# Gate weights and gate inputs of the first recurrence in two parts: three products of 256 columns for each float32 product

## What is computed

```python
def rg_lru(x, w_a, b_a, w_x, b_x, lam):
    xb = x.reshape(B, S, RG_BLOCKS, RG_BLOCK_DIM)
    r = jax.nn.sigmoid(jnp.einsum('bsnc,ncd->bsnd', xb, w_a).reshape(B, S, C) + b_a)
    i = jax.nn.sigmoid(jnp.einsum('bsnc,ncd->bsnd', xb, w_x).reshape(B, S, C) + b_x)
    log_a = -RG_C * r.astype(jnp.float32) * jax.nn.softplus(-lam.astype(jnp.float32))
    a = jnp.exp(log_a)
    mult = jnp.sqrt(-jnp.expm1(2.0 * log_a))
    b = mult * (i * x).astype(jnp.float32)
    _, h = lax.associative_scan(combine, (a, b), axis=1)   # h = a * h_before + b
```

## Time and profile before

| what | value |
|---|---|
| median of 3 runs | 1200.94 us (1200.78 to 1202.69) |
| profiled execution | 1200.8 us |
| its span, first to last instruction | 1199.0 us |
| its mean granted TensorE clock | 0.998 |
| PE, PEld busy | 1181.3 us (99%), 1160.6 us (97%) |
| DVE, ACT, POOL busy | 849.5 us (71%), 713.8 us (60%), 441.5 us (37%) |
| recorded PE products | 10128 |

### The profile page before, as it was taken

How to read it: one execution, slowest core, us unless ns; L and a number is a source line. 1 busy time by engine, 2 the same in 40 slices (tenths; PEclk the granted TensorE clock), 3 DMA queues, 4 the chain that set the end, 5 groups by cost and what they waited for, 6 DMA issues and landing times.

```text
span 1199.0 us, 27004 instructions
## 1 busy us (share of the span) xinstructions
PE 1181.3 (99%) x10128; PEld 1160.6 (97%) x10128; DVE 849.5 (71%) x1399; ACT 713.8 (60%) x1242; POOL 441.5 (37%) x415
## 2 busy tenths in 40 slices
PE   8999999999999999999999999999999999999997
PEld 7999999999999999999999999999999999999996
DVE  5868665676877764878667877755877677877754
ACT  5767667545766654566456666645566456666643
POOL 3007315123344402232338534423622349444422
PEclk9999999999999999999999999999999999999999
DMA  7554445654655666454554655566544554665563
GB/s 260 184 165 159 132 157 164 192 192 159 194 192 192 188 189 197 158 161 147 181 189 140 203 189 193 179 196 182 160 162 155 188 173 151 201 197 191 180 201 100
DMA packets 60286, 212.61 MB, mean 177 GB/s; under 512 B 6688, under 2 KB 7968, under 8 KB 60064
## 3 DMA queue, kind: packets, MB, share of 16 engines
q1 hardware_dynamic: 60192, 211.32, 55.9%
HBM read 210.24 MB, written 1.05 MB: 176 GB/s over the span
## 4 chain that ended last, share of the span: by engine, by line
PE 89%; DVE 5%; issue 2%; ACT 2%; POOL 1%; POOLq 0%; DVEq 0%; ACTq 0%
PE bank L1101 28%; PE bank L1103 28%; PE bank L1102 28%; DVE wlo L1400 2%; PE bank L1117 1%; PE bank L1249 1%; PE bank L1218 1%; ACT whi L766 1%; PE bank L1229 1%; PE bank L1273 1%; DVE prob L1565 1%; DVE prob L1540 0%; POOL u L683 0%; DVE u L1632 0%; PE bank L1158 0%
## 5 line engine op out<-in xcount | busy, mean ns | idle before, releaser
L1400 DVE TENSOR_TENSOR wlo<-raw,whi 128x1024 fp32r<-128x1024 f32 (+1 forms) x400 | 499.9, 1250 | 204.2 <-ACT whi L766 202.5
L1101 PE MATMUL bank<-shifted,whi 128*128 128x256 f32 x2296 | 639.0, 278 | 1.5 <-POOL shifted L702 1.1
L1102 PE MATMUL bank<-shifted,whi 128*128 128x256 f32 x2296 | 636.2, 277 | 0.0
L1103 PE MATMUL bank<-shifted,wlo 128*128 128x256 f32 x2296 | 635.8, 277 | 0.0
L766 ACT ACTIVATE whi<-raw 128x1024 fp32r<-128x1024 f32 (+1 forms) x400 | 416.5, 1042 | 149.4 <-PE bank L1103 137.9
L1101 PEld LDWEIGHTS bank<-shifted,whi 128*128 128x128 f32 x2296 | 431.6, 188 | 3.4 <-POOL shifted L702 1.3
L1103 PEld LDWEIGHTS bank<-shifted,wlo 128*128 128x128 f32 x2296 | 431.7, 188 | 0.0
L1102 PEld LDWEIGHTS bank<-shifted,whi 128*128 128x128 f32 x2296 | 431.1, 188 | 0.0
L662 POOL TENSOR_TENSOR fprod<-ugate,uval 128x256 f32<-128x256 f32 x66 | 95.5, 1447 | 197.5 <-DVE uval L1715 188.2
L1101 PE MATMUL bank<-fhi,whi 128*128 128x256 f32 x528 | 145.8, 276 | 0.0
L1102 PE MATMUL bank<-flo,whi 128*128 128x256 f32 x528 | 145.7, 276 | 0.0
(11 more groups left out here) (218 smaller groups left out, 1258.7 us busy)
## 6 DMA issues: line engine op xcount, KB each, us to landing
raw<-in_w_win SPq DMA_DIRECT2D x140, 512.0 KB, 3.5
raw<-in_w_up SPq DMA_DIRECT2D x132, 512.0 KB, 3.5
raw<-in_w_down SPq DMA_DIRECT2D x48, 448.0 KB, 3.5
raw<-in_w_merge SPq DMA_DIRECT2D x32, 512.0 KB, 3.6
raw<-in_w_out SPq DMA_DIRECT2D x24, 512.0 KB, 4.3
raw<-in_w_down SPq DMA_DIRECT2D x24, 512.0 KB, 3.5
x<-in_x SPq DMA_DIRECT2D x4, 256.0 KB, 4.5
rgw<-in_rg_w SPq DMA_DIRECT2D x1, 1024.0 KB, 10.1
```

The lines of the kernel that those rows point to most:

```text
L1101: pe.matmul(ps, whi[:, slot, w], hi, start=first, stop=False)
L1102: pe.matmul(ps, whi[:, slot, w], lo, start=False, stop=False)
L1103: return pe.matmul(ps, wlo[:, slot, w], hi, start=False, stop=last)
L1400: dve.tensor_tensor(wlo[:, n % RING, w], raw[:, n % RING, w], whi[:, n % RING, w].bitcast(f32), ALU.subtract) \
```

## The change

The gate weights and the eight input tiles are split as all other operands are. `gate_weights(part)` lays the parts over tiles of `yhi` and `ylo` that are not in use until later (eight tiles of each, seen as 16 blocks of 128x128); the parts of the input tiles take turns in `yhi[13]`, `yhi[14]` and `ylo[13]`, `ylo[14]`. ACT copies the weights in two halves of 128x1024 in slots 3 and 4 and tile t in slot 3 + 2t; DVE subtracts the weights' halves in slots 3 and 4 and tile t in slot 4 + 2t. PE's wait of a gate step is now for these parts, and it makes six products in place of two float32 ones. `load_rg` is waited for by ACT, and by PE only at the later `pool_mix`.

```diff
+    for i in range(2):
+        at(3 + i, "rg_weights", i)
     for t in range(KT):
+        at(3 + 2 * t, "rg_x_high", t)
+        at(4 + 2 * t, "rg_x_low", t)
         at(6 + 2 * t, "rg_gates", t)
...
+        def gate_weights(part):
+            at = 17 + 14 * part
+            return shifted[:, at:at + KT, :].rearrange("p t s -> p (t s)").rearrange("p (b n) -> p b n", n=P)
...
# ACT
+            def step_rg_weights(i):
+                if i == 0:
+                    act.wait_ge(load_rg, 32)
+                w = slice(KT * i, KT * (i + 1))
+                act.activation(gate_weights(0)[:, w, :], rgw[:, w, :], ACT.Copy).then_inc(rgw_hi, 1)
+
+            def step_rg_x_high(t):
+                act.wait_ge(conv_done, t + 1)
+                if t >= 2:
+                    act.wait_ge(misc_done, MISC[("rg_gates", t - 2)] + 1)
+                act.activation(yhi[13 + t % 2], u1[:, XR + t, :], ACT.Copy).then_inc(rg_x_hi, 1)
...
# PE
             def step_rg_gates(t):
                 u = MISC[("rg_gates", t)]
                 if t == 0:
-                    pe.wait_ge(load_rg, 32)
-                pe.wait_ge(conv_done, t + 1)
+                    pe.wait_ge(rgw_lo, 2)
+                pe.wait_ge(rg_x_lo, t + 1)
                 wait(pe, misc_read, u)
+                hi, lo = yhi[13 + t % 2], ylo[13 + t % 2]
                 for g in range(2):
-                    mm = pe.matmul(ps_misc[:, g * S:(g + 1) * S], rgw[:, g * KT + t, :], u1[:, XR + t, :], start=True, stop=True,
-                                   skip_group_check=True)
+                    ps, b = ps_misc[:, g * S:(g + 1) * S], g * KT + t
+                    pe.matmul(ps, gate_weights(0)[:, b, :], hi, start=True, stop=False, skip_group_check=True)
+                    pe.matmul(ps, gate_weights(0)[:, b, :], lo, start=False, stop=False, skip_group_check=True)
+                    mm = pe.matmul(ps, gate_weights(1)[:, b, :], hi, start=False, stop=True, skip_group_check=True)
                 mm.then_inc(misc_done, 1)
...
# DVE
+            def step_rg_weights(i):
+                dve.wait_ge(rgw_hi, i + 1)
+                w = slice(KT * i, KT * (i + 1))
+                low(gate_weights(1)[:, w, :], rgw[:, w, :], gate_weights(0)[:, w, :], rgw_lo)
+
+            def step_rg_x_low(t):
+                dve.wait_ge(rg_x_hi, t + 1)
+                low(ylo[13 + t % 2], u1[:, XR + t, :], yhi[13 + t % 2], rg_x_lo)
```

More of the change, by code:

```diff
@@ L331, in build @@
         rg_mixed, rg_driven, rg_state, soft_ready = sem("rg_mixed"), sem("rg_driven"), sem("rg_state"), sem("soft_ready")
+        rgw_hi, rgw_lo, rg_x_hi, rg_x_lo = sem("rgw_hi"), sem("rgw_lo"), sem("rg_x_hi"), sem("rg_x_lo")
         conv_start, tap1, conv_done = sem("conv_start"), sem("tap1"), sem("conv_done")
@@ L930, in _ @@
                      "weights": step_weights, "values": step_values, "diff_sums": step_diff_sums, "diff_norm": step_diff_norm,
+                     "rg_weights": step_rg_weights, "rg_x_high": step_rg_x_high,
                      "rg_gates": step_rg_gates, "rg_gelu": step_rg_gelu, "rg_roots": step_rg_roots,
@@ L1278, in step_pool_mix @@
                 u = MISC[("pool_mix", l)]
+                if l == 0:
+                    pe.wait_ge(load_rg, 32)
                 pe.wait_ge(pooled, l + 1)
@@ L1640, in _ @@
                      "diff_recip": step_diff_recip, "diff_norm": step_diff_norm, "diff_low": step_diff_low,
+                     "rg_weights": step_rg_weights, "rg_x_low": step_rg_x_low,
                      "rg_gates": step_rg_gates, "rg_scan": step_rg_scan,
```

## The result

The changed kernel took 1205.63 us (median of 6 runs, 1203.68 to 1206.30), the kernel before in the same comparison 1201.45 us: a ratio of 1.003, interval 1.002 to 1.004. So it is slower, by 3 to 4 us as the medians have it.

What follows compares the result with a forecast made beforehand. PE, 99% busy, was taken as the bound. On 1200.8 us, 3.6 late at unit 9, less 1.0 for six steps and 0.2 for pace, gave 1203.2; 0.14 for the median made it 1203.3, range 1201.8 to 1205.2.

Steps and rivals of the forecast that it cites:

- The sum: Whole kernel: 3.6 late at unit 9, less 1.0 for six steps and 0.2 for pace, gives +2.4 us.
- unit 9: On PE behind the second gate step: starts at 46.98 instead of 43.38, so 3.6 us late.
- the first of the sum: The starting time: the profiled execution of 1200.8 us, with the median of the runs 0.14 above it.
- The clock rival: PE's first wait: the clock falls there and costs 1.0 more, 1204.4 us, or 1206 with twice the stretch; chance 0.16.
- The first wait: PE at the first gate step waits for DVE's weights and tile 0, starting at 39.37, not 36.00: 3.4 us.
- DVE's slot 3: First weights' half at 33.48, then the wlo of unit 7 at 35.00 behind its whi; DVE free at 36.14.
- The second wait: PE at gate step 1 waits for tile 1 from DVE and starts at 46.29: 0.6 us.
- The saving: Each gate step on PE: six products cost 0.69 to 0.71 instead of 0.86, saving 0.15 to 0.17 us.
- The term for the pace: Unit pairs behind steps t = 2, 4, 6 may run quicker: 0 to 0.46 us, taken at 0.2.
- The rival that DVE stays the bound throughout: All gate steps: tiles 2 to 7 also late, each by up to 0.4, +2.4 again, 1205.7 us; chance 0.06.
- The gain alone: Gate steps: no wait, weights' parts done by 36.00, PE saves 1.3 to 1.9, 1199.0 to 1199.6 us; chance 0.08.

Runs made afterwards that it cites:

- e1: The changed kernel run again with nothing altered, against the kernel before: median 1205.32 us against 1202.29, ratio 1.0024.
- e9: The kernel before with one more PE wait ahead of its first gate step, for the wlo of unit 8: 1206.00 us against 1202.44, ratio 1.0035.
- e2: The changed kernel with twelve products of ones on PE ahead of its wait in the first gate step: 1205.51 us against 1202.29 before, ratio 1.0027.
- e10: The kernel before with PE's two idle times at the start filled with products of ones: 1200.82 us against 1202.44, ratio 0.9991.
- e4: The kernel before with six products on other tiles replacing each gate step's two float32 ones, nothing split: 1200.80 us against 1202.29, ratio 0.9986.
- e7: The changed kernel with weights split ahead of the loop and every tile's steps one slot earlier: 1202.31 us against 1202.89 before, ratio 0.9997.
- e12: The changed kernel with weights split ahead of the loop and only tiles 0 and 1 a slot earlier: 1202.04 us against 1202.44 before, ratio 1.0000.
- e6: The changed kernel with both weights' halves split ahead of the loop, tiles left in place: 1203.15 us against 1202.89 before, ratio 1.0001.
- e5: The changed kernel's added ACT and DVE steps, with PE's float32 gate steps and waits of the kernel before: 1203.62 us against 1202.89 before, ratio 1.0014.
- e3: The changed kernel with the weights' second half and tile 0 ahead of prepare_sum on DVE in slot 4: 1204.39 us against 1202.29 before, ratio 1.0021.
- e11: e12 with PE's two idle times at the start filled as in e10: 1200.62 us against 1202.44 for the kernel before, ratio 0.9993.

## Why the prediction was right or wrong

**The direction and the mechanism were right.** PE waits once long and once short for DVE's subtraction, as walked, and from 50 us on DVE has room. The sum was +2.4; unit 6 to 22 shows +2.5, and the groups +2.7 and +3.1. That the sum came within 0.1 is in part luck: unit 9 was 3.3 late where I had 3.6, and behind it 0.8 came back where I had 1.2, two errors that cancel.

**The forecast of 1203.3 was low for the median of 1205.63**, which is also 0.4 over the range. (As a difference it is +4.2 over the 1201.45 measured beside it; the range reached to +4.3 over the 1200.94 that I had.) The profiled execution of the changed kernel, at 1203.7, and the lower group, at 1203.4, are what the sum describes. The step that failed for the time was the first of the sum: it stood on one profiled execution and three runs of before as if the kernel had one time, though one of the three, 1202.69, lay in the upper group. It has two, 2.2 us apart, and a median of six runs is one or the other by chance; that both profiled executions fell in the lower group was chance as well. The mean granted clock of a run mostly tells them apart (0.998 or 0.999 in the lower group of the kernel before, 0.995 to 0.997 in the upper), but only that of the one profiled execution was read.

**The clock rival** gave 1204.4 to 1206 and so seems to have named the time. It did not: in the profiled executions with PE idle for 2.8 to 2.9 us in the first wait (after, e1, e9) the granted clock stays at 1.00 there, and filling the gap (e2) changes nothing. The price that I read from the earlier trace rows for a low clock, 1.6, is near the 2.2 that it costs at the start. There the idle time that the earlier trace rows shows, which I took as proof that a gap of 1.7 is harmless, is part of what lets it fall in some two thirds of the executions. One execution that got through was no proof. The Trainium skill, "TensorE: Matmul & The Clock Gate", section "Why this matters for your kernels", asks for no long idle gaps between bursts. The traces agree in that filling idle time kept the clock up (e10), but not on which gap matters: the long one, 2.9 us behind dense work, did not bring it down, while one of 1.8 with few products behind it did (e1, e2 and e9 at 16 us).

**The first wait**: 3.4 forecast, 3.06 measured. The step that was off is DVE's slot 3. I had the `wlo` of unit 7 start at 35.00 because its `whi` would end at 34.97. I had miscounted ACT's units: the `whi` at 30.99 in the earlier trace rows is that of unit 7, and the one at 33.92 of unit 8. The heading of the earlier trace rows has the same slip. So DVE did not wait there; the `wlo` started at 34.6 (35.05 less the late start), 0.4 earlier. For the same reason ACT's first added half came ahead of the result of unit 4 and pushed it from 30.71 to 31.27 (31.73 less the late start), which made nobody wait. The durations from the earlier trace rows were exact (1.23, 0.42, 1.62 for `prepare_sum`); the hand-over to PE took 0.14 and not 0.05.

**The second wait**: 0.6 forecast, 0.43 measured. From the start of gate step 0 to that of step 1 the walk had 6.92 and the trace has 6.80; PE wanted step 1 6.37 behind the start of step 0 and not some 6.27, because a step behind a wait takes 0.79 and not 0.69. Late at unit 9: 3.6 forecast, 47.12 - 43.38 - 0.46 = 3.3 measured.

**The saving**: 0.165 a step and 0.2 for pace, forecast; behind unit 9 the changed kernel got 0.8 back where I had 1.2. A step of 0.86 became one of 0.72, so 0.14 for each of six. The term for the pace gave nothing: the rounds go at 6.30 where before they went at 6.36 and 6.52 in turn, and the two units in them take 5.58, the mean of before. The products alone gave 1.9 (e4), with the quicker pace all through; with the real tiles it is some 1.0 over all eight steps (e7 and e12 with their waits taken off).

**The rival that DVE stays the bound throughout** is out; in 70 to 80 us DVE has 6.87 of 10. **The gain alone** is what e4 shows, 50.0 from 6 to 22, and would have needed free DVE time ahead of 36 us. e6 shows where such time lay: at 20.8 to 23.5 us, earlier in the queue.

## What to carry to other kernels

Where the bound engine is fed by another that is some 95% busy over a stretch (DVE from 30 to 50 us), cheaper work on the bound engine that needs more on the feeder can cost more than it gives there: 2.3 us of subtraction in the wrong two slots cost 2.3 of the 2.5 us lost, and were nearly free some 12 us earlier. The order on the feeder's queue decides, not its share over the span; taking the wait off (e5) or cutting it in pieces (e3) changes only where it shows. And before a difference of 0.2% is forecast, the kernel's own runs are to be looked at for groups, by their clocks.

## What the runs showed of the hardware that was not expected

- PE's granted clock went to 0.50 for 3 to 7 us in the profiled executions of e1, e2, e4, e9 and e12. Ahead of it stood an idle time of 1.8 us, twelve products in 2.7 us, and another idle time of 0.7 to 1.1. In e1, e2 and e9 it fell among the twelve products, at 15.9 to 16.4 us, so behind the first idle time alone; in e4 and e12 at the end of the second, at 18.3 to 18.9. It cost 1.5 to 2.5 us in units 0 and 1 (9.5 to 10.5 in place of 8.0). With products of ones in both idle times none of 11 runs was in the upper group, nor any of 11 of e11. A single idle time of 2.8 to 2.9 us behind 15 us of dense products did not bring it down in any of the three profiled executions that had one.
- A POOL subtraction on 128x256 elements (0.74 us) held back the DVE operation beside it until it was through or nearly so: 0.17 became 0.63, 0.42 became 0.91.
- Streams of the same products run at 113 to 115 or at 117 to 119 ns each. Ahead of the first gate step all kernels run at the quicker. Before, the two units behind every other gate step ran at the slower; in the changed kernel the first 25 to 40 products behind each gate step did. Float32 products are thus not needed for it. In e4, whose gate products read other tiles, the slower did not occur from unit 7 to 22. No run settles what sets it.
